# Reordering the start, the angle chain, the last hidden block of an MLP group, the differential turn and the last two weight units of a two-block transformer kernel

## The reference, cut to what matters

```python
h = rms_norm(x, g_mix); proj = h @ w_in                  # block 1, with rotary tables from sin/cos
o_diff = rms_norm(diff_attention(...), g_diff_sub) * (1 - lambda_init)
x = x + concatenate([out_mla, out_diff]) @ w_out
hm = rms_norm(mem, g_mem); xk = hm @ w_xk; xv = hm @ w_xv # memory keys and values
x = x + (silu(hf @ w_gate) * (hf @ w_up)) @ w_down        # MLP, hidden width 5632, once per block
...
gate = sigmoid(rms_norm(x, g_ple) @ w_ple_gate + b_ple_gate)
x = x + (p @ w_ple_proj) * gate                           # last step of block 2
```

## Time and profile before

| | us |
|---|---|
| median of 3 runs | 2423.7 (2423.31 to 2424.94) |
| the profiled execution | 2422.88 |
| its span (first to last instruction) | 2421.1 |
| PE matmuls busy | 2392.8 (99% of the span, 10880 matmuls) |
| DVE busy | 1698.2 (70%) |
| ACT busy | 1134.2 (47%) |
| DMA | 461.96 MB, mean 191 GB/s |

### The profile page before, as it was taken

The page is one execution under the profiler, slowest core; times in us unless marked ns, Lnnn a source line. Parts: engine busy times, 40 slices in busy tenths (PEclk is TensorE's granted clock), DMA queues, the critical chain, the costliest instruction groups (busy, mean ns, idle before and its releaser), DMA issues.

```text
span 2421.1 us, 31550 instructions
## 1 busy us (share of the span) xinstructions
PE 2392.8 (99%) x10880; PEld 1992.0 (82%) x10880; DVE 1698.2 (70%) x2276; ACT 1134.2 (47%) x1525; POOL 10.4 (0%) x23
## 2 busy tenths in 40 slices
PE   8999999999999999999999999999999999999999
PEld 7988878888888788887888888888888878888787
DVE  7778677666567746668897976777556765667875
ACT  6554545544344434445544445454444443444553
POOL 0000000000000000000000000000000000000000
PEclk9999999999999999999999999999999999999999
DMA  8655545565666555665566564565656566565554
GB/s 306 222 169 179 166 156 174 169 205 191 192 192 190 191 192 182 203 195 176 182 199 194 181 217 162 191 200 183 201 190 199 179 198 196 191 194 189 191 186 163
DMA packets 125994, 461.96 MB, mean 191 GB/s; under 512 B 14000, under 2 KB 14128, under 8 KB 125120
## 3 DMA queue, kind: packets, MB, share of 16 engines
q1 hardware_dynamic: 123360, 446.75, 56.7%
q0 software_dynamic: 2384, 13.68, 1.6%
q10 hardware_dynamic: 144, 0.07, 0.0%
HBM read 458.35 MB, written 2.10 MB: 190 GB/s over the span
## 4 chain that ended last, share of the span: by engine, by line
PE 92%; DVE 7%; ACT 1%; issue 0%; DMA 0%; SPq 0%; ACTq 0%; DVEq 0%
PE acc L452 87%; DVE w_lo L1217 3%; PE acc L457 2%; DVE heads L1352 1%; DVE tmp_c L1352 1%; PE acc L625 1%; PE po L671 1%; PE pt L516 1%; PE po L663 1%; ACT w_hi L798 0%; PE pt L642 0%; PE acc L609 0%; DVE tmp_c L1834 0%; DVE tmp_a L1337 0%; DVE tmp_a L1341 0%
## 5 line engine op out<-in xcount | busy, mean ns | idle before, releaser
L1217 DVE TENSOR_TENSOR w_lo<-raw,w_hi 128x1024 fp32r<-128x1024 f32 x844 | 1023.8, 1224 | 612.1 <-ACT w_hi L798 602.3
L798 ACT ACTIVATE w_hi<-raw 128x1024 fp32r<-128x1024 f32 x844 | 891.2, 1059 | 1086.5 <-PE acc L452 995.7
L452 PE MATMUL acc<-w_hi,norm_hi 128*128 128x512 f32 (+1 forms) x2240 | 872.6, 390 | 0.5 <-issue 0.5
L452 PE MATMUL acc<-w_hi,norm_lo 128*128 128x512 f32 (+1 forms) x2240 | 868.8, 388 | 0.0
L452 PE MATMUL acc<-w_lo,norm_hi 128*128 128x512 f32 (+1 forms) x2240 | 596.6, 388 | 0.1
L452 PEld LDWEIGHTS acc<-w_hi,norm_hi 128*128 128x128 f32 x2240 | 420.6, 188 | 86.1 <-issue 0.9
L452 PEld LDWEIGHTS acc<-w_lo,norm_hi 128*128 128x128 f32 x2240 | 419.0, 188 | 87.7 <-DVE w_lo L1217 1.8
L452 PEld LDWEIGHTS acc<-w_hi,norm_lo 128*128 128x128 f32 x2240 | 420.6, 188 | 85.4
L452 PE MATMUL acc<-w_hi,mix_hi 128*128 128x512 f32 x1088 | 426.2, 392 | 12.3 <-DVE mix_lo L1314 7.9
L452 PE MATMUL acc<-w_hi,mix_lo 128*128 128x512 f32 x1088 | 424.4, 390 | 0.0
L452 PE MATMUL acc<-w_lo,mix_hi 128*128 128x512 f32 x1088 | 291.4, 390 | 0.0
(11 more groups left out here) (212 smaller groups left out, 896.9 us busy)
## 6 DMA issues: line engine op xcount, KB each, us to landing
raw<-stream SPq DMA_DIRECT2D x844, 512.0 KB, 3.5
x<-x_tok POOLq DMA_DIRECT2D x2, 2048.0 KB, 10.4
heads<-x_in POOLq DMA_DIRECT2D x4, 512.0 KB, 6.6
x<-mem_tok POOLq DMA_DIRECT2D x2, 1024.0 KB, 7.5
heads<-rows_in POOLq DMA_DIRECT2D x2, 1024.0 KB, 7.2
heads<-decay_in POOLq DMA_DIRECT2D x4, 512.0 KB, 5.1
heads<-mem_in SPq DMA_DIRECT2D x3, 512.0 KB, 9.9
out<-x SPq DMA_DIRECT2D x3, 512.0 KB, 5.0
```

Source lines behind the costliest of these rows:

```text
L452: last = pe.matmul(acc[:, slot, c * NB:c * NB + width], a[:, k * T + c * P:k * T + (c + 1) * P], w[:, s, kk * width:(kk + 1) * width], sta ...
L798: act.activation(w_hi[:, (units.fixed - 1) % RING, :], src, ACT.Copy).then_inc(w_hi_ready, 1)
L1217: dve.tensor_tensor(w_lo[:, s, :], src, w_hi[:, s, :].bitcast(F32), ALU.subtract)\
```

## The change

1. **Start.** The first memory part is taken chunk by chunk (`MEM_STEPS`), and ACT makes the first unit's `w_hi` in two halves. PE waits for the first half (`first_half_ready`) and the first chunk, does that chunk's 4 matmuls, then waits for the second. ACT now waits for the unit's load (`take_raw`) ahead of the first chunk.
2. **Angle chain.** ACT does unit 6 ahead of the Exp, and units 7 and 8 ahead of the Sin. DVE does unit 6 ahead of the chain and unit 7 in its middle.
3. **Hidden squares.** For the last block of a group of 4, DVE does all 16 squares first, then two units, `hidden_low`, three units. ACT does `hidden_hi` one unit earlier.
4. **Differential turn.** The second half's mean and root come one unit earlier, ahead of the first half's `kept_low`; `diff_scale(1)` one unit earlier; PE's turn behind unit 6 in place of 7; `kept_hi` and `kept_low` one unit earlier.
5. **End.** PE does the last two units together, all 12 matmuls of token tile 0 first and then those of tile 1 (`last_units`). DVE's order behind them is: bias 0, gate 0, bias 1, add 0, gate 1, add 1.

```diff
+        MEM_STEPS = ((0, 1, 0), (1, 2, 0), (2, 4, 1), (4, 8, 2), (8, 12, 3), (12, 16, 4))
...  one_block (PE)
+                    if halves and ki == 0:
+                        pe.wait_ge(first_half_ready, 1)
+                        pe.wait_ge(operand_ready, 1)
+                        passes(((w_hi, act_hi), (w_hi, act_lo)), True, (0,))
                     pe.wait_ge(w_hi_ready, units.value())
                     if need:
                         pe.wait_ge(*need(ki))
-                    if by_tile and ki == n_units - 1:
...
-                    passes(((w_hi, act_hi), (w_hi, act_lo)), True)
+                    passes(((w_hi, act_hi), (w_hi, act_lo)), True, *([(1,)] if halves and ki == 0 else []))
...
+            def last_units(act):
+                act_hi, act_lo = act
+                slot, first = (blocks.fixed - 1) % 2, units.fixed
+                for t in range(TT):
+                    for u in range(2):
+                        s = (first + u) % RING
+                        if t == 0:
+                            units.add()
+                            pe.wait_ge(w_hi_ready, units.value())
+                            pe.wait_ge(raw_read, units.value())
+                        for kk in range(UK):
+                            k = (NU - 2 + u) * UK + kk
+                            for w, a in ((w_hi, act_hi), (w_hi, act_lo), (w_lo, act_hi)):
+                                last = pe.matmul(...)
+                    last.then_inc(tile_used, 1)
...  output projection (PE)
-                    3: lambda: turn_diff(0), 7: lambda: turn_diff(1)})
+                    3: lambda: turn_diff(0), 6: lambda: turn_diff(1)})
...  mlp (ACT)
-                        split(2)
+                        split(1)
                         if b == 0 and n == CB:
                             hidden_hi(n - 1)
+                        split(1)
...  start (ACT)
-            for i, n in enumerate((1, 1, 2, 1, 1)):
-                mem_hi(i)
+            src = take_raw()
+            for half, ready in enumerate((first_half_ready, w_hi_ready)):
+                mem_hi(half)
+                at = half * NB
+                act.activation(w_hi[:, 0, at:at + NB], src[:, at:at + NB], ACT.Copy).then_inc(ready, 1)
+            units.add()
+            for i, n in enumerate((1, 2, 1, 1)):
+                mem_hi(2 + i)
                 split(n)
+            split(1)
             wait_rows()
             act.activation(lam[:, 2:4], lam[:, 2:4], ACT.Exp).then_inc(func_ready, 1)
-
+            split(2)
             wait_rows()
             act.activation(tmp_c[:, SINES], tmp_c[:, SINES], ACT.Sin).then_inc(func_ready, 1)
-            split(5)
+            split(2)
...  output projection (ACT)
-                               5: lambda: column_root(r_head[:, 1, 0:4]),
-                               7: lambda: kept_hi(12, "g_diff_sub", (0, 1, 0, 1))})
+                               4: lambda: column_root(r_head[:, 1, 0:4]),
+                               6: lambda: kept_hi(12, "g_diff_sub", (0, 1, 0, 1))})
...  mlp (DVE)
                         elif b == 0 and n == CB:
-                            split(1)
-                            turn_hidden(range(2))
-                            split(1)
-                            turn_hidden(range(2, 4)).then_inc(hidden_turned, 1)
+                            turn_hidden(range(4)).then_inc(hidden_turned, 1)
+                            split(2)
+                            hidden_low(n - 1, tmp_c[:, :])
                             split(3)
-                            hidden_low(n - 1, tmp_c[:, :])
...  start (DVE): split(1) ahead of the angle chain, split(1) in its middle, split(2) for split(4) behind it
...  output projection (DVE)
-            output("g_xattn", {0: lambda: diff_scale(0), 4: lambda: kept_low(8, "g_diff_sub", (0, 1, 0, 1)),
-                               5: lambda: head_mean(2 * P, EPS_DIFF, DIFF_H, 1, 4), 6: lambda: diff_scale(1),
-                               8: lambda: kept_low(12, "g_diff_sub", (0, 1, 0, 1)), 9: lambda: scale_memory(XV)})
+            output("g_xattn", {0: lambda: diff_scale(0), 4: lambda: (head_mean(2 * P, EPS_DIFF, DIFF_H, 1, 4),
+                                           kept_low(8, "g_diff_sub", (0, 1, 0, 1))),
+                               5: lambda: diff_scale(1), 7: lambda: kept_low(12, "g_diff_sub", (0, 1, 0, 1)),
+                               9: lambda: scale_memory(XV)})
...  end (DVE)
+            last_biased(0)
+            last_gated(0)
+            last_biased(1)
+            last_added(0)
+            last_gated(1)
+            last_added(1)
```

More of the change, by code:

```diff
@@ L217, in two_blocks @@
         w_hi_ready = sem("w_hi_ready")
+        first_half_ready = sem("first_half_ready")
         raw_read = sem("raw_read")
@@ L424, in one_block @@
             def one_block(n_units, act, k0=0, token_major=False, need=None, mid=None, width=NB, per=UK,
-                          by_tile=False, part=None, back=0):
+                          part=None, back=0, halves=False):
                 mids = mid or {}
@@ L442, in one_block, with passes @@
                     s = (units.fixed - 1) % RING
-                    def passes(pairs, first, tiles=range(TT if token_major else CB)):
-                        for c in tiles:
-                            for kk in range(min(per, KC - ki * per)):
+                    def passes(pairs, first, kks=range(min(per, KC - ki * per))):
+                        for c in range(TT if token_major else CB):
+                            for kk in kks:
                                 k = k0 + ki * per + kk
@@ L481, in one_block @@
                         mids[ki]()
+            def last_units(act):
[11 more added lines that the diff above has]
+                            for w, a in ((w_hi, act_hi), (w_hi, act_lo), (w_lo, act_hi)):
+                                last = pe.matmul(acc[:, slot, t * NB:(t + 1) * NB],
+                                                 a[:, k * T + t * P:k * T + (t + 1) * P],
+                                                 w[:, s, kk * NB:(kk + 1) * NB], start=False, stop=u == 1,
+                                                 skip_group_check=True)
+                    last.then_inc(tile_used, 1)
             def scores_read(n):
@@ L692, in _ @@
             pe.matmul(po[:, 1, 0:2], ones[:, :], lam[:, 0:2], start=True, stop=True).then_inc(sums_done, 1)
-            one_block(NU, mix, token_major=True, need=lambda ki: (operand_ready, ki + 1 if ki < 2 else ki // 2 + 2))
+            one_block(NU, mix, token_major=True, need=lambda ki: (operand_ready, ki + 2 if ki < 2 else ki // 2 + 3),
+                      halves=True)
             one_block(NU, mix, token_major=True)
-            one_block(NU, norm, token_major=True, need=operand_need(NBD + 1))
-            operands.add(2 * NBD + 1)
+            one_block(NU, norm, token_major=True, need=operand_need(NBD + 2))
+            operands.add(2 * NBD + 2)
             one_block(U_KV, norm, token_major=True, width=KV_W, per=KV_K,
@@ L702, in _ @@
             lat = Q_LAT // P // UK
-            one_block(lat, mix, need=lambda ki: (operand_ready, 2 * NBD + 2))
+            one_block(lat, mix, need=lambda ki: (operand_ready, 2 * NBD + 3))
             one_block(lat, mix, mid={0: lambda: turn(of_block(tmp_b), (block_taken, 4), n=3, kept=True)})
             for i in range(4):
-                one_block(1, mix, k0=CB, token_major=i >= 2, need=lambda ki: (operand_ready, 2 * NBD + 3))
+                one_block(1, mix, k0=CB, token_major=i >= 2, need=lambda ki: (operand_ready, 2 * NBD + 4))
             one_block(lat, mix, token_major=True)
@@ L768, in _ @@
                 one_block(NU, norm, token_major=True, need=lambda ki: (operand_ready, base + NBD + (ki * UK >= 12)),
-                          by_tile=b == NBD - 1)
+                          part=range(NU - 2) if b == NBD - 1 else None)
+            last_units(norm)
             assert units.fixed == UNITS
@@ L1023, in mem_hi @@
             def mem_hi(i):
-                act.wait_ge(mem_landed[i], 16)
-                for c in range(*MEM_PARTS[i]):
+                at, end, landed = MEM_STEPS[i]
+                act.wait_ge(mem_landed[landed], 16)
+                for c in range(at, end):
                     last = act.activation(chunks(mix_hi, c, 1), chunks(heads, MEM_IN + c, 1), ACT.Copy,
@@ L1185, in _ @@
             for t in range(TT):
[L1186 to L1189, removed]
+                act.wait_ge(tile_taken, t + 1)
                 act.activation(tile_of(tmp_b, t), tile_of(tmp_a, t), ACT.Sigmoid).then_inc(func_ready, 1)
@@ L1591, in mem_low @@
                 dve.wait_ge(hi_ready, his.add())
-                for c in range(*MEM_PARTS[i]):
+                for c in range(*MEM_STEPS[i][:2]):
                     last = dve.scalar_tensor_tensor(out=chunks(mix_lo, c, 1), in0=chunks(heads, MEM_IN + c, 1),
@@ L1599, in x_low @@
```

(20 more changed lines are left out.)

## The result

| | before | after |
|---|---|---|
| median of 6 runs, us | 2423.61 (2422.69 to 2428.72) | 2409.06 (2408.47 to 2409.61) |
| ratio | | 0.9936, 95% interval 0.9924 to 0.9949 |
| profiled execution, us | 2422.88 | 2408.47 |
| its span, us | 2421.1 | 2406.7 |

The kernel is faster, by 14.6 us from median to median, by 15.5 us if one goes by the ratio of all runs (which one run of before with 2428.72 moves). I had forecast 13.1. So the direction is right and every named stall went as told, but 1.5 us or more of gain were missing from the sum. The span, which the sum puts at 2408.0, is 2406.7 here and 2407.4 in two further profiles of the changed kernel.

What follows compares the result with a forecast made beforehand. PE was taken as the bound, so only its idle time could be won: 9.0 + 1.85 + 1.5 + 0.7 + 0.0 = 13.1 us off 2423.7 gave a median of 2410.6 us, range 2408.9 to 2413.5 (chance 0.82).

Steps and rivals of the forecast that it cites:

- the sum: Whole kernel: the five savings add to 13.1 us, median 2410.6 us; chance 0.70 that it comes as told, 2409.8 to 2412.0.
- What bounds: Whole kernel: PE's matmuls are busy 2392.8 of 2421.1 us, so at most 28.3 us of idle time can be won.
- Hidden squares: Down projections, four places: PE's wait for `mix_lo` of L1314 goes, 2.25 us each, 9.0 us saved; bounds 0 and 9.0.
- the restart: PE's first unit after a squares stall: takes 2.84 us and not 2.72, so 0.12 us is added to each 2.13 us stall.
- Angle chain: Near 27 us: PE's wait for `w_hi` of unit 6, held behind the Sin, goes; 1.85 us saved, bounds 0 and 1.85.
- Differential turn: Output projection: two stalls, 3.15 us together, become one of 1.6 us; 1.5 us saved, bounds 0 and 3.15.
- End: Behind PE's last matmul: tile 0's gate is done earlier, shortening the final chain; 0.7 us saved, bounds 0.6 and 0.8.
- Start: First unit: PE starts at 7.01 in place of 7.04 and nothing is won; 0.0 us, bounds -0.1 and possibly +2.4.
- The rival of the clock's rise: Start: PE's clock rises at another moment, 0.20 us per matmul more or fewer at slow pace; 2409.4 to 2413.0, chance 0.06.
- loads late behind the squares: Down projections: SP's loads of units 8 and 9 take over 9.4 us, half of 9.0 lost; 2415.1 us, chance 0.06.
- nothing won: Down projections: the stall moves whole from `mix_lo` to `w_lo` and the loads; 2419 to 2424 us, chance 0.02.
- slower: Down projections: the same loads take longer still, from 12.7 us each on; at 14 us each 2429 us, chance 0.02.

Runs made afterwards that it cites:

- E: Kernel before with DVE's `mix_lo` of the last hidden block one unit later in all four places: 2436.34 us, 12.7 us slower than before.
- experiment D: Kernel before with the angle part alone: 2421.89 us against 2423.64 before, ratio 0.9994 (0.9985 to 1.0003).

## Why the prediction was right, and where it was wrong

- **What bounds.** Right: PE, and only its idle stretches could be won. Its matmuls are the same 10880.
- **Hidden squares.** The mechanism and the 2.13 us of each stall were right, and the covers held (2.7 us for `mix_lo`). The term of the sum that was mis-sized is the restart: "a restart costs 0.12 more". That row is one execution in which the clock did not fall behind any of the four stalls. In others it falls behind such a stall, and the restart costs 1.6 + 0.12. The term was 9.0 us; it measured 10.3 alone (7.5 to 14.1) and 10.1 undone. By counting falls (3 in 20 stalls of 2 us, 1.6 us each) an execution has 4 x 0.15 x 1.6 = 1.0 us of it, which fits; the count is small. That the stall lets the clock fall is shown by E, where longer stalls do it every time.
- **Angle chain.** Right in the rows (1.83 against 1.85), the load of unit 6 was there in time, and what queued behind it was hidden. Behind its stall the clock can fall too (once in the five profiles that have the stall), which my 1.85 lacks; how much that is on the median, experiment D is too coarse to say.
- **Differential turn.** Right: a stall of 1.51 us stayed (1.6 forecast), the second went; 1.69 by the profiles, 1.2 by medians, 1.5 forecast.
- **End.** Right: 0.69 by the profiles against 0.7.
- **Start.** Right that nothing is won: 0.0 alone (within 2 us), 0.2 undone. The profile shows 0.98, and that is the clock's rise. Had I taken the profile after at its word I would have called this step wrong. One reading in it is a little off: not all 12 matmuls of unit 0 ran at 0.427 before. The last four took 1.49 us, from 10.62 to 12.11, and not 1.71, so the pace rose within them. The rival of the clock's rise was named with the right bounds, yet it moves single runs and not the median.
- **The sum.** 13.1 forecast, 14.6 measured. The clock's falls behind the squares (about 1.0 to 1.3) make up most of the difference; the remaining few tenths, among them the falls behind the angle stall, are within what the medians tell (before alone was 2423.6 to 2424.3 from set to set). Between the fastest runs of the two kernels on record, 2421.45 and 2408.47, lie 13.0 us: where the clock falls least, the sum comes out as it was. My range had its lower edge only 1.7 under the forecast for want of this term. The one profile of before that I had showed no fall behind a stall; the spread of its runs and their mean clock (0.999 to 0.996 in the later sets) do.
- **The other rivals** (loads late behind the squares, nothing won, slower) did not come. ACT did wait up to 2.4 us for these loads, as that rival said, but had over six to spare.

The Trainium skill's page "TensorE: Matmul & The Clock Gate", section "HAM oscillation — how this bites in real kernels", says that a wait between groups of matmuls can make the gate throttle again, so that the next group starts at half rate. I cited that page for the start alone and should have held its rule against the stalls: for the 3.7 us waits the trace here agrees four times of four; for those of 2.0 us three times in twenty, with 1.6 us each.

## What to carry to other kernels

A short stall of a TensorE that is otherwise always busy costs more than the gap in one profile: take several profiles, look behind each gap for matmuls at twice the spacing, and add chance times price. Compare the mean clock of all runs and not only that of the profiled one: run times that go up in step with a falling mean clock are a sign of it. With all the changed kernel's parts in, the spread went (51 runs of before: 2421.45 to 2428.39; 16 of the changed kernel: 2408.47 to 2409.82), but no single part did that alone: 2.9 us were left with only the squares stalls removed, 1.8 us with all parts but these. Don't credit an edit with a gain in the first microseconds before a second profile shows the clock rising at the same moment.

## What the hardware showed that was not expected

The clock's rise at the start moved: unit 1 started anywhere from 11.1 to 12.5 us in profiles of kernels whose PE started at 7.0 to 7.3. After a stall of 1.97 us it fell only 0.8 to 1.2 us into the work that followed; after one of 3.69 us it was low at once or within 0.5 us. The same happens in the cross attention, which the change doesn't touch: windows of the changed kernel's first profile

```profile
405.00:410.00 5.00, 4.16 (x20) 3.19 (x18) 3.50 (x7) 2.59 (x7) 0.00 (x0) 1.00 0.40 138
410.00:415.00 5.00, 2.85 (x12) 2.34 (x13) 3.77 (x13) 4.21 (x15) 0.00 (x0) 0.76 0.21 84
```

have it at 0.76 between 410 and 415 us, while its third profile has 1.00 there. Six of the 14 profiles have such a fall, the first one of before among them (0.57 from 418 to 422 us). It makes this stretch 0.8 to 0.9 us longer (the chain goes from 386.05 to 424.06 in the first profile of before, from 385.70 to 422.79 in the second), and it hardly touches the comparison of the two first profiles, since both have it. Why all three falls behind the 2 us stalls came at the first of the four places stays open; three are too few to call it a rule.
